# Two-layer hybrid block on one core: second branch, output products and second input by row halves; step product with few stationary columns

## What is computed

```python
ya = (ya * jax.nn.silu(za)) @ w_a_o
yb = (yb * jax.nn.silu(zb)) @ w_b_o
merged = jax.nn.sigmoid(ga) * ya + jax.nn.sigmoid(gb) * yb
x = rms_norm(x + gate[:, None] * (merged @ w_out), final_g)
...
proj = jnp.einsum('bsd,de->bse', x, w_in[layer])
q, k, v, z_att, z_ssm, xbc, dt_raw = jnp.split(proj, list(SPLITS), axis=-1)
xbc = jax.nn.silu(causal_depthwise_conv(xbc, conv_w[layer], conv_b[layer]))
dt = jax.nn.softplus(dt_raw + dt_bias[layer])
```

## Time and profile before

| | us |
|---|---|
| median of three executions | 2242.68 |
| lowest and highest | 2241.42, 2246.37 |
| the profiled execution | 2240.73 |
| its span, first to last instruction | 2239.0 |

### The profile page before, as it was taken

The page is one execution under the profiler, slowest core; times in us unless marked ns, Lnnn a source line. Parts: engine busy times, 40 slices in busy tenths (PEclk is TensorE's granted clock), DMA queues, the critical chain, the costliest instruction groups (busy, mean ns, idle before and its releaser), DMA issues.

```text
span 2239.0 us, 27588 instructions
## 1 busy us (share of the span) xinstructions
PE 2025.1 (90%) x10892; PEld 1028.8 (46%) x10892; DVE 1227.9 (55%) x2318; ACT 810.9 (36%) x1358; POOL 620.0 (28%) x638
## 2 busy tenths in 40 slices
PE   3999889988999988696998998999999999999796
PEld 2434335444444555244444665544544444454442
DVE  6428999899992465305454888201433333343516
ACT  3313434433216654113213443312344444334503
POOL 0031416542842022756232224021012012202240
PEclk8999999998999999898999999999999999999998
DMA  7110111211411212213211002011101100110301
GB/s 320 38 47 24 43 38 57 76 65 54 164 38 57 95 38 95 97 54 125 83 38 38 1 1 76 25 51 38 38 1 38 38 14 25 38 39 1 114 19 75
DMA packets 18528, 129.74 MB, mean 58 GB/s; under 512 B 1760, under 2 KB 1760, under 8 KB 13024
## 3 DMA queue, kind: packets, MB, share of 16 engines
q1 hardware_dynamic: 12864, 99.67, 12.0%
q0 software_dynamic: 5536, 28.31, 3.2%
HBM read 109.10 MB, written 18.87 MB: 57 GB/s over the span
## 4 chain that ended last, share of the span: by engine, by line
PE 74%; DVE 15%; ACT 4%; issue 3%; POOL 3%; DMA 2%; SPq 0%; DVEq 0%; POOLq 0%; ACTq 0%
PE ps L804 47%; PE ps L801 7%; PE ps L857 5%; PE ps L842 4%; PE ps L872 3%; DVE arena L1441 3%; POOL arena L504 1%; PE ps L1034 1%; PE ps L1054 1%; DVE small L1611 1%; DVE arena L1599 1%; ACT arena L1224 1%; PE ps L922 1%; POOL arena L634 1%; DVE small L1598 1%
## 5 line engine op out<-in xcount | busy, mean ns | idle before, releaser
L804 PE MATMUL ps<-hT,W 128*128 128x512 bf16 x3456 | 817.7, 391 | 43.8 <-ACT arena L1195 29.7
L804 PEld LDWEIGHTS ps<-hT,W 128*128 128x128 bf16 x3456 | 326.4, 97 | 498.4 <-issue 37.2
L513 POOL TENSOR_TENSOR W<-W 128x512 bf16<-128x512 f32 x224 | 247.7, 1144 | 453.7 <-DMA W<-in_loads 452.5
L804 PE MATMUL ps<-W,arena 128*128 128x512 bf16 x1152 | 262.8, 389 | 20.0 <-DVE arena L1775 19.6
L1450 DVE COPY arena<-ps 128x512 f32<-128x512 f32 (+3 forms) x288 | 147.3, 551 | 238.3 <-PE ps L872 238.0
L1464 DVE CUSTOM_DVE_ANT_0 arena<-ps,arena 128x128 f32<-128x128 f32 (+7 forms) x192 | 138.4, 755 | 202.9 <-PE ps L857 182.8
L1224 ACT ACTIVATE arena<-arena,small 128x128 f32<-128x128 f32 (+7 forms) x192 | 147.4, 768 | 173.6 <-DVE small L1464 173.3
L504 POOL TENSOR_TENSOR arena<-arena 128x512 f32<-128x512 f32 (+1 forms) x80 | 133.3, 1666 | 219.2 <-ACT arena L1376 126.3
L804 PEld LDWEIGHTS ps<-W,arena 128*128 128x128 bf16 x1152 | 111.1, 97 | 170.8 <-DVE arena L1775 20.1
L1231 ACT ACTIVATE arena<-arena,small 128x128 f32<-128x128 f32 (+7 forms) x192 | 138.2, 767 | 116.2 <-DVE small L1475 116.2
L872 PE MATMUL ps<-ck,arena 128*128 128x128 f32 x864 | 124.9, 277 | 25.1 <-DVE arena L1450 19.6
(11 more groups left out here) (289 smaller groups left out, 2265.4 us busy)
## 6 DMA issues: line engine op xcount, KB each, us to landing
W<-in_loads SPq DMA_DIRECT2D x35, 2048.0 KB, 7.9
gates_scratch<-arena SPq DMA_DIRECT2D x32, 256.0 KB, 2.0
arena<-gates_scratch POOLq DMA_DIRECT2D x2, 4096.0 KB, 13.3
arena<-in_x SPq DMA_DIRECT2D x2, 2048.0 KB, 13.6
W<-in_mods SPq DMA_DIRECT2D x2, 2048.0 KB, 18.3
hT<-in_mods SPq DMA_DIRECT2D x2, 2048.0 KB, 28.8
arena<-in_x POOLq DMA_DIRECT2D x1, 4096.0 KB, 13.7
x_scratch<-arena POOLq DMA_DIRECT2D x8, 512.0 KB, 6.6
```

Source lines behind the costliest of these rows:

```text
L513: last = nc.gpsimd.tensor_tensor(low(v), v, high(v), ALU.subtract)
L804: last = mm(o, left[:, :, a], right[:, :, b], start=(k == 0 and (a, b) == PRODUCTS[0]), stop=(k == steps - 1 and (a, b) == PRODUCTS[-1]))
```

## The change

- bo's units are ordered by row half: all eight feature tiles of rows 0 to 511, then of rows 512 to 1023. PE begins the out products when the first eight low halves are made, and waits for the rest before the ninth out unit.
- DVE splits out0 before the whole loop of low halves, and no longer before the fifteenth.
- The out units go by row half: rows 0 to 511 with out0 and out1, then rows 512 to 1023 with both (`OUT_ORDER`). So SP can issue xbc0's load after the twelfth out unit.
- ACT's squares and roots, and DVE's scalings, follow in that order; the squares go into a place of their own (`x2_junk`).
- PE turns groups 0 to 3 after the fourteenth out unit and 4 to 7 after the fifteenth. Then come the first row halves of channel tiles 0 and 1, then groups 8 to 15, then the second row halves.
- POOL splits xbc0 in runs of three, three and two pieces between its last out sums.
- dt has no load of its own. Its 16 columns ride in unused columns of the first load ("small"); DVE copies them into `dt_weights` and splits them early on. SP's third load waits for that too.
- dt's product has these 16 columns stationary and rows moving: two units of 24 matmuls of 512 columns, then a third that turns the 16 x 1024 result back in eight small blocks. It comes after channel tile 3, with the small steps of ACT and DVE behind it.

```diff
-             "zb", "ao", "gb1", "gate0", "gate1", "bo", "out0", "out1", "dt", "xbc0", "xbc1", "xbc2", "zs0", "zs1"]
+             "zb", "ao", "gb1", "gate0", "gate1", "bo", "out0", "out1", "xbc0", "xbc1", "xbc2", "zs0", "zs1"]
...
+OUT_ORDER = [(f"out{c}", 4 * half + t) for half in range(2) for c in range(2) for t in range(4)]
...
+    units[a:a + 16] = OUT_ORDER
+    a = first["xbc0"]
+    units[a:a + 4] = [("xbc0", i) for i in (0, 2, 1, 3)]
+    a = first["xbc1"]
+    first = {name: u + 3 * (u >= a) for name, u in first.items()}
+    first["dt"] = a
+    units[a:a] = [("dt", i) for i in range(3)]
...
+                    if n == 2:
+                        sp.wait_ge(s_dtw, 1)
...
+                if 12 <= i < 15:
+                    split("xbc0", (0, 3, 6, 8)[i - 12:i - 10])
             nc.gpsimd.dma_start(dist, alibi[0]).then_inc(s_alibi, 16)
             nc.gpsimd.dma_start(nlog, alibi[1]).then_inc(s_alibi, 16)
-            split("dt")
-            split("xbc0")
...
+                if name == "dt":
+                    return KD, [(full, lambda k: parts(dt_weights[:, k, :]), lambda k: acts(hT, k, half, 512))]
...
-                if name == "dt":
-                    return KD, [(slice(t * 16, t * 16 + 16), lambda k, t=t: acts(hT, k, t * P, P),
-                                 lambda k: weights(KD, k, 0, 16)) for t in range(NT)]
...
+                if name == "dt" and i == 2:
+
+                    pe.wait_ge(s_free, FIRST["dt"] + 2)
+                    for t in range(NT):
+                        last = nc.tensor.transpose(ps[:, unit_bank(u), t * 16:t * 16 + 16], dtT[0:16, t * P:(t + 1) * P],
+                                                   ident[0:16, 0:16])
...
-            pe.wait_ge(s_mlow, 16)
-            units("out0")
-            units("out1")
-
-
-            turn_tiles(XR, s_x2, 4, s_xt2, s_ht2)
+            def turn_x2(some):
+
+                for n in some:
+                    k, half = turned(n)
+                    if k == 0:
+                        pe.wait_ge(s_x2, 4 * half + 4)
+                    if n >= 4:
+                        pe.wait_ge(s_ht2, n - 3)
+                    for j in range(4):
+                        last = nc.tensor.transpose(ps[:, 4 + n % 4, j * P:(j + 1) * P],
+                                                   XR[:, 4 * half + j, k * P:(k + 1) * P], ident)
+                    last.then_inc(s_xt2, 1)
+
+            pe.wait_ge(s_mlow, 8)
+            for idx in range(16):
+                if idx == 8:
+                    pe.wait_ge(s_mlow, 16)
+                unit(FIRST["out0"] + idx)
+                if idx == 13:
+                    turn_x2(range(0, 4))
+                if idx == 14:
+                    turn_x2(range(4, 8))
+            pe.wait_ge(s_ht2, 8)
+            unit(FIRST["xbc0"])
+            unit(FIRST["xbc0"] + 1)
+            turn_x2(range(8, 16))
             pe.wait_ge(s_ht2, 16)
-            units("dt")
+            unit(FIRST["xbc0"] + 2)
+            unit(FIRST["xbc0"] + 3)
...
+                if ct == 4:
+                    units("dt")
...
+            def x2_norm(t):
+
+                act.wait_ge(s_comb, 41 + OUT_ORDER.index(("out1", t)))
+                if t >= 2:
+                    act.wait_ge(s_x2n[0], t - 1)
+                A(x2_junk[t % 2], XR[:, t, :], ACT.Square, accum_out=ss[:, t:t + 1]).then_inc(s_x2n[0], 1)
+                act.wait_ge(s_x2n[1], t + 1)
+                A(rs[:, t:t + 1], rs[:, t:t + 1], ACT.Sqrt).then_inc(s_x2n[2], 1)
...
+            for idx in range(16):
+                evac(FIRST["out0"] + idx)
+                if idx >= 1 and OUT_ORDER[idx - 1][0] == "out1":
+                    x2_norm(OUT_ORDER[idx - 1][1])
+                if idx == 13:
+                    x2_high(range(0, 4))
+                if idx == 14:
+                    x2_high(range(4, 8))
+            x2_norm(7)
+            evac(FIRST["xbc0"])
+            evac(FIRST["xbc0"] + 1)
+            x2_high(range(8, 16))
+            evac(FIRST["xbc0"] + 2)
+            evac(FIRST["xbc0"] + 3)
...
+            dve.wait_ge(s_w[0], 16)
+            link(V.tensor_copy(dt_weights, W[:, 0, :].rearrange("p (k n) -> p k n", k=KD)[:, :, 200:216]))
+            V.tensor_tensor(low(dt_weights), dt_weights, high(dt_weights), ALU.subtract).then_inc(s_dtw, 1)
...
+            split_out("out0")
             for i in range(16):
-                if i == 14:
-                    split_out("out0")
                 dve.wait_ge(s_comb, 25 + i)
-                m = mT[:, i // 2, (i % 2) * 512:(i % 2) * 512 + 512]
+                m = mT[:, i % 8, (i // 8) * 512:(i // 8) * 512 + 512]
...
+            for t in range(5):
+                x2_rows(t)
+            x2_low(range(0, 4))
+            x2_rows(5)
+            x2_low(range(4, 8))
+            x2_rows(6)
+            x2_rows(7)
+            x2_low(range(8, 16))
...
-        "small": np.concatenate([at["k"], at["ki"], at["v"], at["wi"]], axis=1),
+        "small": np.concatenate([at["k"], at["ki"], at["v"], at["wi"], dt2], axis=1),
```

More of the change, by code:

```diff
@@ L242, in layer_kernel @@
         bgate = area(19968, 1024)
+        x2_junk = [area(20992 + 1024 * s, 1024) for s in range(2)]
         BH = area(15872, 1024, "p (r g s q) -> p r g s q", r=2, g=BATCH_PAIRS, s=SUB)
@@ L504, in mult, with split @@
                 return nc.gpsimd.tensor_tensor(o, a, b, ALU.mult)
-            def split(name):
+            def split(name, pieces=(0, 8)):
                 n = LOADS.index(name)
@@ L510, in split @@
                 w = W[:, n % 2, :]
-                for a in range(0, LOADW, 512):
+                for a in range(512 * pieces[0], 512 * pieces[1], 512):
                     v = w[:, a:a + 512]
                     last = nc.gpsimd.tensor_tensor(low(v), v, high(v), ALU.subtract)
-                last.then_inc(s_pack, 1)
-                pool.wait_ge(s_pack, SPLIT_LOADS.index(name) + 1)
+                if pieces[1] == 8:
+                    last.then_inc(s_pack, 1)
+                    pool.wait_ge(s_pack, SPLIT_LOADS.index(name) + 1)
             pool.wait_ge(s_prv, 3)
@@ L786, in unit @@
                     return
-                rows_ = slice(0, 72 if name == "small" and i < 2 else P)
+                if name == "dt" and i == 2:
[3 more added lines that the diff above has]
+                                                   ident[0:16, 0:16])
+                    last.then_inc(s_unit, 1)
+                    return
+                rows_ = slice(0, 72 if name == "small" and i < 2 else 16 if name == "dt" else P)
                 steps, pieces = operands(name, i)
@@ L1017, in _ @@
             for ct in range(CONV_TILES):
-                for half in range(2):
-                    unit(FIRST["xbc0"] + 2 * ct + half)
+                if ct == 4:
+                    units("dt")
+                if ct >= 2:
+                    for half in range(2):
+                        unit(FIRST[f"xbc{ct // 4}"] + 2 * (ct % 4) + half)
                 if 2 <= ct < 12:
@@ L1160, in evac @@
                 elif name in ("ao", "bo", "out0", "out1"):
-                    c = {"ao": 8, "bo": 24, "out0": 40, "out1": 48}[name] + i
+                    q = i if name[0] != "o" else OUT_ORDER.index((name, i))
+                    c = {"ao": 8, "bo": 24}.get(name, 40) + q
                     act.wait_ge(s_comb, max(c - 3, 8))
-                    last = A(tmp[i % 4], bank, ACT.Copy)
+                    last = A(tmp[q % 4], bank, ACT.Copy)
                 elif name == "q":
@@ L1171, in evac @@
                 elif name == "dt":
-                    last = A(dtr, bank[:, 0:128], ACT.Copy)
+                    last = A(dtT[0:16, half], bank[0:16], ACT.Copy) if i < 2 else A(dtr, bank[:, 0:128], ACT.Copy)
                 elif name[:3] == "xbc":
@@ L1320, in _ @@
             act.wait_ge(s_comb, 40)
-            evacs("out0")
-            for t in range(NT + 1):
-                if t < NT:
-                    evac(FIRST["out1"] + t)
-                if t >= 1:
-                    act.wait_ge(s_comb, 48 + t)
-                    A(hT[:, t - 1, :], XR[:, t - 1, :], ACT.Square, accum_out=ss[:, t - 1:t]).then_inc(s_x2n[0], 1)
-                    act.wait_ge(s_x2n[1], t)
-                    A(rs[:, t - 1:t], rs[:, t - 1:t], ACT.Sqrt).then_inc(s_x2n[2], 1)
@@ L1333, in _ @@
-            for n in range(16):
-                act.wait_ge(s_xt2, n + 1)
-                k, half = turned(n)
-                A(high(hT[:, k, half * 512:half * 512 + 512]), ps[:, 4 + n % 4, :], ACT.Copy)\
-                    .then_inc(s_h2, 1)
-            evacs("dt")
-            act.wait_ge(s_dtv, 1)
-            link(A(dtv, dtv, ACT.Exp, scale=-1.0))
-            A(aexp, par("alog"), ACT.Exp)
-            A(dtv, dtv, ACT.Ln, bias=1.0).then_inc(s_dta, 1)
+            def x2_norm(t):
[5 more added lines that the diff above has]
+                A(rs[:, t:t + 1], rs[:, t:t + 1], ACT.Sqrt).then_inc(s_x2n[2], 1)
@@ new lines, in x2_high @@
+            def x2_high(some):
```

(19 more changed lines are left out.)

72 lines of the change are left out of this document (45 added, 27 removed).

## The result

| | before | after |
|---|---|---|
| median, first comparison | 2243.82 | 2224.02 |
| median, second comparison | 2247.13 | 2225.21 |
| the profiled execution | 2240.73 | 2221.81 |
| its span | 2239.0 | 2220.0 |

The ratio is 0.9912 [0.9895, 0.9929] in the first comparison and 0.9898 [0.9878, 0.9918] in the second. The ratio goes by all executions and can differ a little from the quotient of the medians. The change makes the kernel faster by some 20 to 22 us. The forecast was 2216 from a median of 2242.68, a ratio of 0.9881; its sum of 25.6 us is a ratio of 0.9886. So the sign and most of the size were right, and some 4 to 6 us of the gain are missing. The first comparison's median lies 0.02 us above the upper end of the forecast's range, 2224.0; by the ratio of the second it would be 2219.8 of 2242.68, inside it.

The account below looks back on a forecast made before the run. PE's row of products bounds the kernel, with holes of 19.56 us before the out products, 12.88 in the turns, and dt's short matmuls. Terms of 15.4, 14.1 and 0.3 less 4.1 and rounding gave 25.6, so 2216; range 2207.5 to 2224.

Parts of the forecast that it names:

- sum of 25.6 us: Gain at the xbc stage's end: 15.4 at the out products, 14.1 at the turns, 0.3 clock, less 4.1 and rounding.
- The split against gated_low: Before bo: DVE's split of out0 holds POOL's last gated_low; PE starts bo 4.75 us later and loses 2.0 to the clock.
- Rival (a): Before bo: POOL's gated_low gets in first or is not held up, 6.75 us better, 2209; chance 0.17.
- bo by halves, out units without a stop: From bo into the out products PE waits for nothing; out1's split has slack 3.5 us; gain 15.4 at the out products.
- The turns: Turned groups between out and xbc units: 14.1 us gained, with 6.8 us left between the second and third xbc unit.
- The dip of 1.0 us: Behind the turns, in the xbc stage: a clock dip costing 1.0 us, bounds 0 and 2.5.
- Rival (b): Tail of the out products: POOL's pieces hold DVE's scalings, perhaps out1's split; 3 to 6 us, 2219 to 2222; chance 0.13.
- The step product: dt after channel tile 3: 10.8 us for 48 matmuls, 12.2 in all against 8.1 before, a loss of 4.1.
- (d): In dt: the product with 16 stationary columns leaves the clock at its lower level, +10.8 us, 2227; chance 0.05.
- Carrying the gain to the end: Behind the xbc stage: PE's own units release everything later, so the gain of 25.6 us arrives unchanged.
- (c): In the out products: PE still stops, since ACT evicts none before all sixteen sums; 13 us late gives 2220; chance 0.03.
- (e): From bo's late start the clock falls to 1.2 GHz and stays; ten units at that level give 2270; chance 0.03.

Follow-up runs that it names:

- lock edit: The changed kernel with one wait more: DVE splits out0 only when POOL has made its last gated low half; 2215.72, ratio 0.9866.

## Why the forecast was right where it was, and where it was not

Times below count from PE's last attention group, which takes the executions' different fronts out.

| step | forecast | measured |
|---|---|---|
| bo begins | 7.85 | 7.37 |
| bo ends | 53.3 | 53.4 |
| first xbc unit | 143.7 | 143.3 |
| third xbc unit | 161.3 | 160.8 |
| dt, all | 12.2 | 12.3 |
| xbc stage ends | 302.0 | 300.9 |

*The split against gated_low.* DVE got in first by 0.23 us (879.04 against 879.27), POOL was held for 4.67 us, and with POOL let in first the middle is 6.3 us shorter; the sum had 6.75. The trace agrees with the rule of the Trainium skill (SBUF — State Buffer, "Who interferes with whom") that a VectorE instruction with two SBUF inputs and a GpSimd instruction that reads SBUF lock each other out, and the order of issue decides who waits. A POOL instruction of 0.40 us took 4.67 us, beside a DVE instruction of 4.68 us that had begun first. Rival (a) was the other outcome of this race. It did not happen. The kernel in which it does has a ratio of 0.9866, or 2212.6 of the 2242.68 on which the 2209 stood: the loss behind the stage is in it too.

*bo by halves, out units without a stop.* Right: no stop came. Out1's split ended at 948.5, with the fifth unit due at 951.6; a slack of 3.1 for 3.5. Once PE starts bo 4 us sooner, as with the lock edit, the slack is gone.

*The turns.* The waits inside the out units were met, and the first eight groups cost nothing but themselves. The 6.8 us between the second and third xbc unit were there (1037.43 against 1030.79, 6.6). The dip of 1.0 us that I put behind them did not come: four units took 21.6 us (1037.43 to 1059.05). That is most of the 1.1 us by which the xbc stage ended early. Rival (b) fell: the scalings took 1.28 to 2.19 us, and that some executions came out near its 2219 to 2222 has another cause.

*The step product.* 48 matmuls of 16 stationary and 512 moving columns took 10.98 us, 0.229 each, as wide ones do: the estimate of 10.8 was right, and (d) fell. What I misjudged is the comparison. I took the old form at the 8.1 us of its old place and called the new one a loss of 4.1. But in the kernel before a third of that was a stop, as the second half of the unit shows, and in the new place the old form takes 4.95.

```profile
1062.27 1.19 PE L804 MATMUL ps<-W,hT 128*128 128x16 bf16 x39 [2.85 <-issue]
```

Against 4.95 the new form loses some 6.7 us in the middle. The forecast of the time is not touched by this, but a reader of it would have kept the wrong half of the edit.

*Carrying the gain to the end.* This is the step of the forecast that failed: "everything later is released by PE's own units, so I carry what is gained at the end of xbc ... unchanged to the end". The sum put nothing there. Measured, 27.0 us were gained in the middle and 21.9 arrived by the medians of the second comparison, 19.8 by those of the first: 5 to 7 us were lost outside it. That the miss is no larger is luck, for the middle gained 1.4 us more than the sum had.

One part of the loss is a wait that PE's own units do not release. The order of the later units did not change; their numbers did, and the bank of a unit is made from its number. The diff says so in its line `u + 3 * (u >= a)`, where the name dt had counted one. It costs a wait of 1.5 us. The wait is in every trace of a kernel with three dt units and the old rule for the bank, and in the kernel before once the bank is moved, and in no other. With the bank moved back the ratio is 0.9887, and the forecast's 25.6 us are 0.9886; with an interval of 0.0018 to either side, that they meet so closely is chance.

The rest is a term that my sum did not have at all, the granted clock outside the stretch that I looked at. Executions of one kernel differ by it: those of the kernel before run from 2240.7 us at a mean granted clock of 0.964 to 2251.6 at 0.959. Both traced executions of before lie at the fast end of that (2240.73 and 2240.35 against a median of 2247.2). Of the three of after, 2221.81 was the fastest of its four, and 2225.04 and 2224.91 lie at the median. So the 6 to 9 us that the traces show behind the xbc stage are partly a matter of which execution was traced, and the medians are the better measure of the loss. The traced fronts also differ, by 1.3 to 5.7 us. It is not the early copy of dt's weights: the same matmuls start 1.2 us earlier after than before at 439 us, and 1.4 later at 580, and between them PE's idle time is only 0.5 us longer, and the rest is busy time of the same matmuls; the kernel with the row halves alone, which has no such copy, has a front of 878.23. Each of the twelve traces of a changed kernel has a longer front than the two of before, so some of the loss may lie there; why is not shown.

I had given the medians' uncertainty 1 us to either side. Two comparisons of the same changed kernel gave ratios 0.0014 apart, 3 us. That term was too small, and the upper end of the range, 2224.0, has no room for it; 2224.02 lies outside.

Rivals (c) and (e): no stop in the out units, and, but for the first 11 us of bo, no stretch of products at the lower clock; both fell.

Still open: why the falls in the second attention come more often in some executions, and how much of that the wait for the bank brings about.

## What to carry to other kernels

Where banks, buffers or semaphore values are worked out from a running number, a change in how many units a stage counts moves everything behind it; list who shares a resource with whom before and after, to the last unit. Cost a new form of an operation against the old form in the new place, without the stops that the old place gave it. A gain read from one traced execution is only as good as that execution's place among the others: look at the mean clock of several before giving a range of less than a few us.

## What the runs showed of the hardware that I had not expected

- 192 matmuls with 128 stationary and 16 moving columns ran in 4.95 us, 26 ns each with their weight loads beside them; 48 with 16 stationary and 512 moving took 10.98 us. For the same product the narrow side is better the moving one here. The granted clock hardly changed this: in the kernel before, 153 of the narrow ones took 4.22 us, 28 ns each, with 0.56 granted (1055 to 1060 us), against 26 ns with 1.00 in the new place.
- With a stop of 5.26 us before bo the granted clock was 0.73 over the first 11 us, and bo took 3.0 us longer; after one of 1.22 us it stayed at 1.00.
- Falls of the granted clock far from any edit decide several us: in the tail, twelve falls with some 59 us at the lower level after against nine with 45 before, and PE's busy time for the same matmuls is 5.2 us longer. Their number differs between executions of one kernel too: ten to twelve in the three traces of after.
